# The triangular inverse of a gated DeltaNet head: four doubling levels moved from 96 by 96 products to 32 by 32 diagonal blocks

## What is computed

```python
    kk = jnp.einsum('bhncd,bhnsd->bhncs', k, k)
    A = jnp.where(strict, beta[..., :, None] * kk * decay_mat, 0.0)
    rhs = jnp.concatenate([v * beta[..., None], k * (beta * jnp.exp(gam))[..., None]], axis=-1)
    sol = lax.linalg.triangular_solve(A, rhs, left_side=True, lower=True, unit_diagonal=True)
```

```python
    for gi in range(N_EXPERT_GROUPS):
        hdn = (jax.nn.silu(jnp.einsum('nd,edf->nef', xt, w_gate[gi]))
               * jnp.einsum('nd,edf->nef', xt, w_up[gi]))
        hdn = hdn * comb[:, gi, :, None].astype(hdn.dtype)
        y = y + jnp.einsum('nef,efd->nd', hdn, w_down[gi])
```

## Time and profile before

| | us |
|---|---|
| median of 3 runs | 849.45 (849.22 to 850.07) |
| the profiled execution, its own time | 850.3 |
| its span, first to last instruction | 848.6 |
| PE busy in the span | 786.8 |
| DVE, ACT, POOL busy | 327.2, 309.3, 132.0 |

### The profile page before, as it was taken

One profiled execution on the slowest core, in us unless ns is written; L12 is line 12 of the kernel. 1 busy time (PEld: TensorE's weight loads), 2 busy tenths in 40 slices (PEclk: granted clock), 3 DMA queues, 4 the chain that ended last, 5 costly groups with the idle time before them and its releaser, 6 DMA issues.

```text
span 848.6 us, 14904 instructions
## 1 busy us (share of the span) xinstructions
PE 786.8 (93%) x5989; PEld 581.5 (69%) x5989; DVE 327.2 (39%) x735; ACT 309.3 (36%) x593; POOL 132.0 (16%) x148
## 2 busy tenths in 40 slices
PE   3889999999999999999999999999999888988885
PEld 2778999999999999746556565565655554554542
DVE  3462777768675775327111221112211121121112
ACT  4561755776665646313212212121221211112123
POOL 3172262243156234200000000000000000000000
PEclk9885999999999999999999999999999999999998
DMA  9413434233514432689999999999999999999992
GB/s 321 121 51 100 112 100 112 76 89 85 152 28 117 119 103 75 248 328 410 422 427 425 421 429 422 428 424 423 429 421 429 422 427 423 427 426 422 427 419 119
DMA packets 84091, 240.99 MB, mean 284 GB/s; under 512 B 7089, under 2 KB 65570, under 8 KB 67506
## 3 DMA queue, kind: packets, MB, share of 16 engines
q1 hardware_dynamic: 83554, 238.34, 71.9%
q10 hardware_dynamic: 464, 1.64, 0.5%
HBM read 238.92 MB, written 1.05 MB: 283 GB/s over the span
## 4 chain that ended last, share of the span: by engine, by line
PE 74%; DMA 15%; SPq 3%; ACT 2%; DVE 2%; issue 2%; POOL 0%; ACTq 0%; DVEq 0%; POOLq 0%
PE banks L1616 20%; PE banks L1911 18%; DMA ring<-in_expert_w_up_dram 14%; PE banks L1962 10%; PE banks L1792 3%; PE banks L1922 3%; PE banks L1853 3%; PE banks L1724 2%; PE banks L1726 2%; PE banks L1707 2%; SPq L635 2%; SPq L641 1%; ACT bench L972 1%; PE banks L1673 1%; PE banks L1779 1%
## 5 line engine op out<-in xcount | busy, mean ns | idle before, releaser
L1911 PE MATMUL banks<-ring,bench 128*64 128x256 f32 x2048 | 229.8, 380 | 16.6 <-DMA ring<-in_expert_w_up_dram 10.6
L1911 PEld LDWEIGHTS banks<-ring,bench 128*64 128x64 f32 x2048 | 150.5, 137 | 104.8 <-issue 26.0
L1616 PE MATMUL banks<-rounded 128*128 128x272 f32 (+2 forms) x1368 | 207.3, 302 | 2.9 <-DVE rounded L1190 2.8
L1616 PEld LDWEIGHTS banks<-rounded 128*128 128x128 f32 (+1 forms) x1368 | 181.7, 194 | 6.3 <-DVE rounded L1190 3.0
L1962 PE MATMUL banks<-ring,bench 128*64 128x512 f32 x512 | 116.9, 599 | 11.6 <-ACT bench L972 11.6
L1530 DVE TENSOR_TENSOR bench<-banks,bench 128x256 f32<-128x256 f32 x32 | 13.6, 425 | 244.5 <-PE banks L1911 181.5
L1962 PEld LDWEIGHTS banks<-ring,bench 128*64 128x64 f32 x512 | 34.0, 137 | 74.0 <-issue 54.5
L983 ACT ACTIVATE ysb<-banks 64x512 f32<-64x512 f32 x63 | 37.2, 591 | 119.4 <-PE banks L1962 118.6
L972 ACT ACTIVATE bench<-banks 128x256 f32<-128x256 f32 x32 | 12.3, 383 | 180.1 <-PE banks L1943 180.1
L773 ACT ACTIVATE rounded<-room 128x1024 fp32r<-128x1024 f32 x56 | 58.6, 1052 | 14.8 <-PE banks L1616 14.7
L1190 DVE TENSOR_TENSOR rounded<-room,rounded 128x1024 fp32r<-128x1024 f32 x42 | 55.4, 1321 | 17.4 <-ACT rounded L773 16.2
(11 more groups left out here) (270 smaller groups left out, 960.1 us busy)
## 6 DMA issues: line engine op xcount, KB each, us to landing
ring<-in_expert_w_gate_dram SPq DMA_DIRECT2D x32, 2048.0 KB, 30.9
ring<-in_expert_w_down_dram SPq DMA_DIRECT2D x64, 1024.0 KB, 29.4
ring<-in_expert_w_up_dram SPq DMA_DIRECT2D x31, 2048.0 KB, 32.1
room<-in_w_in_dram SPq DMA_DIRECT2D x56, 512.0 KB, 3.8
ring<-in_w_out_dram SPq DMA_DIRECT2D x8, 512.0 KB, 4.3
ring<-in_expert_w_up_dram SPq DMA_DIRECT2D x2, 1024.0 KB, 36.9
x<-in_x_dram ACTq DMA_DIRECT2D x2, 512.0 KB, 4.6
poolw<-in_pool_w_dram SPq DMA_DIRECT2D x4, 256.0 KB, 4.2
```

The costliest lines, as they stand in the source:

```text
L1616: ins = T.matmul(o, a, b[:, k, lo_at:L], start=(k == 0 and n == 0), stop=(k == KT - 1 and n == 2))
L1911: ins = T.matmul(pb[5 + c][half * 64:half * 64 + SLOTS, 0:256], xgT[:, q % ROOMS, kt, j * SLOTS:(j + 1) * SLOTS], w[:, kt, half * 256:(hal ...
```

## The change

The levels 2, 4, 8 and 16 only ever touch the three 32 by 32 blocks on the diagonal of each 96 by 96 matrix. The change keeps those blocks alone, stacked on the partitions: partitions 0 to 31, 32 to 63 and 64 to 95 hold the first, second and third diagonal block of a chunk, and a chunk takes 32 columns instead of 96.

- `AT`, `at`, `tb` and `ub` go. Instead ACT copies the diagonal blocks of A (step `ac`, three instructions of 32 by 96), and DVE makes the first T and, with a transpose of 32 by 32 blocks, its transpose U (step `base`, three instructions of 96 by 96).
- A level of the first four is now: POOL masks 96 by 96 elements instead of 96 by 288; PE forms `W` in nine 32 by 32 matmuls, three chunks times three blocks, each on its own diagonal quadrant of the array; ACT copies 96 by 96; PE forms the transpose of Y (`YT`) in nine such matmuls; DVE adds it to U (step `uc`) and transposes the sum to get T (step `tf`). Y itself is no longer formed.
- At level 16 `uc` writes the blocks into the full U, and levels 32 and 64 need one product `W`, one `YT`, one copy (`uc`) and, for level 32, one transpose (`tf`).
- The planner's costs are changed with the steps, and the orders come out anew.
- POOL makes more constants at the start, and clears two buffers.

No DMA is added or taken away, and SP's order is the same.

```diff
+LEVEL = 0.43
...
-            op(("X", h, lv), "pe", 0.51 if big else 0.2 if lv == 4 else 0.33,
-               when(("mask", h, lv) if big else None, ("tb", h) if lv == 0 else ("ty", h, lv - 1)), due(h, left - 1), gets=("X", h, lv))
+            op(("W", h, lv), "pe", LEVEL if inner else 0.2, when(("mask", h, lv) if inner else None, ("base", h) if lv == 0 else ("uc", h, min(lv - 1, 3))), due(h, left - 1), gets=("W", h, lv))
...
+                    for r in range(3):
+                        rows = slice(32 * r, 32 * r + 32)
+                        nc.scalar.activation(Ac[rows, h % 2], Ab[rows, h % 2, :, rows], ACT.Copy).then_inc(S("ac"), 1)
...
+            for r in range(3):
+                rows = slice(32 * r, 32 * r + 32)
+                chain(nc.gpsimd.tensor_copy(blows[rows, 0, :], mlow[rows, rows]))
+                chain(nc.gpsimd.tensor_copy(blows[rows, 1:1 + MASKED, :], lows[rows, :, rows]))
+                chain(nc.gpsimd.tensor_copy(unit[rows, :], ident[rows, rows]))
+            for t in (Uf, Th):
+                chain(nc.gpsimd.memset(t, 0.0))
...
-                nc.gpsimd.tensor_tensor(OTb[:, h % 2, lv % 2], ATb[:, h % 2], mup[:, 1 + lv:2 + lv, :].to_broadcast([CH, NC_, CH]), ALU.mult).then_inc(S("OT"), 1)
+                nc.gpsimd.tensor_tensor(Ob[:, h % 2, lv % 2], Ac[:, h % 2], blows[:, 1 + lv:2 + lv, :].to_broadcast([CH, NC_, 32]), ALU.mult).then_inc(S("OT"), 1)
...
-                    chain(V.tensor_tensor(tmpT[:, 0], Ab[:], spread(mlow), ALU.mult))
+                    chain(V.tensor_tensor(Tmp[:, 0], Ac[:, h % 2], blows[:, 0:1, :].to_broadcast([CH, NC_, 32]), ALU.mult))
...
+                    chain(V.tensor_tensor(Tc[:, h % 2], Tmp[:, 0], unit.rearrange("p (o t) -> p o t", o=1).to_broadcast([CH, NC_, 32]), ALU.add))
+                    V.transpose(out=Uc[:, h % 2], in_=Tc[:, h % 2]).then_inc(S("base"), 1)
...
+                    if lv < 3:
+                        takes(V.tensor_tensor(Uc[:, h % 2], c3(p[0:CH, 0:CH]), Uc[:, h % 2], ALU.add), ("YT", h, lv))
...
+                    if lv < 3:
+                        ins = V.transpose(out=Tc[:, h % 2], in_=Uc[:, h % 2])
...
+            def per_block(key, product):
+
+                p = bank(pe, key)
+                for c in range(NC_):
+                    for r in range(3):
+                        rows = slice(32 * r, 32 * r + 32)
+                        ins = product(p[rows, c * 32:(c + 1) * 32], c, rows)
+                fills(ins, key)
...
-                if kind == "AT":
-                    h = step[1]
-                    taken(pe, ("G", h))
-                    per_chunk(("AT", h), CH, CH, lambda o, c: T.transpose(o, Ab[:, c, :], ident[0:CH, 0:CH]))
...
-                        per_chunk(("X", h, lv), CH, CH, lambda o, c: T.matmul(o, OTb[:, h % 2, lv % 2, c, :], Tb[:, h % 2, c, :], start=True, stop=True))
+                        per_block(("W", h, lv), lambda o, c, rows: T.matmul(o, Ob[rows, h % 2, lv % 2, c, :], Uc[rows, h % 2, c, :], start=True, stop=True, skip_group_check=True))
...
-                    if lv < MASKED and kind == "Y":
-                        per_chunk(("Y", h, lv), CH, CH, lambda o, c: T.matmul(o, Ub[:, h % 2, c, :], Xb[:, h % 2, c, :], start=True, stop=True))
-                    elif lv < MASKED:
-                        per_chunk(("YT", h, lv), CH, CH, lambda o, c: T.matmul(o, Xb[:, h % 2, c, :], Ub[:, h % 2, c, :], start=True, stop=True))
+                    if lv < MASKED:
+                        per_block(("YT", h, lv), lambda o, c, rows: T.matmul(o, Tc[rows, h % 2, c, :], Wc[rows, h % 2, c, :], start=True, stop=True, skip_group_check=True))
```

More of the change, by code:

```diff
@@ L345 @@
 OT_AT = {step[1:]: n + 1 for n, step in enumerate(s for s in SEQ_OF["pool"] if s[0] == "mask")}
+TF_AT = {step[1:]: n + 1 for n, step in enumerate(s for s in SEQ_OF["dve"] if s[0] == "tf")}
 LO_AT = {}
@@ L1329, in _ @@
+                if kind == "tf":
                     h, lv = step[1:]
-                    b = LEVELS[lv]
-                    q = filled(dve, ("YT", h, lv))
-                    if lv < MASKED:
-                        takes(V.tensor_tensor(Ub[:, h % 2], c3(q[0:CH, 0:LP]), Ub[:, h % 2], ALU.add), ("YT", h, lv))
-                    else:
-                        takes(V.tensor_copy(Ub[0:b, h % 2, :, b:b + 32], c3(q[0:b, 0:LP])[:, :, b:b + 32]), ("YT", h, lv))
+                    taken(dve, ("YT", h, lv))
+                    if lv < 3:
+                        ins = V.transpose(out=Tc[:, h % 2], in_=Uc[:, h % 2])
+                    elif lv == 3:
+                        if h >= 2:
+                            filled(dve, ("YT", h - 2, 5))
+                        for r in range(2):
+                            rows = slice(32 * r, 32 * r + 32)
+                            ins = V.transpose(out=Th[rows, h % 2, :, rows], in_=Uf[rows, h % 2, :, rows])
+                    else:
+                        ins = V.transpose(out=Th[32:64, h % 2, :, 0:32], in_=Uf[0:32, h % 2, :, 32:64])
+                    ins.then_inc(S("tf"), 1)
@@ L1708, in _ @@
                     else:
-                        p = bank(pe, ("X", h, lv))
-                        for c in range(NC_):
-                            ins = T.matmul(p[b:b + 32, c * CH:c * CH + b], ATb[0:b, h % 2, c, b:b + 32], Tb[0:b, h % 2, c, 0:b],
-                                           start=True, stop=True, skip_group_check=True)
-                        fills(ins, ("X", h, lv))
-                if kind in ("Y", "YT"):
+                        b = LEVELS[lv]
+                        low, diag = slice(0, b), slice(b, b + 32)
```

161 lines of the change are left out of this document (73 added, 88 removed).

## The result

| | before | after |
|---|---|---|
| median of 4 runs, us | 849.34 (847.32 to 850.07) | 818.72 (816.84 to 821.12) |
| profiled execution: time, span, us | 850.3, 848.6 | 820.57, 818.8 |

The ratio is 0.9645 (interval 0.9607 to 0.9682): 30.6 us faster, where the sum of the forecast had 12.7. The sign came out as predicted and so did the mechanism of the middle stretch. The size did not, the reading of the first head did not either, and the time lies outside the range.

What follows compares the result with a forecast made beforehand. The prediction took PE to pace the mixers and the weight stream to keep the experts' stage's length. Its terms, 11.9 + 2.5 - 1.7 = 12.7 us, taken from 849.45, gave 837 us, with 828 to 851 for 8 in 10.

Steps and rivals of the forecast that it cites:

- PE bounds the middle: From 90 to 357 us PE is full, so a microsecond less PE work is close to a microsecond less time.
- The price of a small group: Eighteen records on three quadrants cost PE 0.60 us, between 0.50 and 0.68; a head saves 2.0 us.
- The share of 85%: Seven heads where PE is full: of 14.0 us saved, 11.9 get through, because smaller groups have waits with less filling.
- The first head: A chain through DVE, ACT and PE before the middle stretch; shorter copies and additions save 2.5 us, between 1 and 4.
- a risk of the other sign: Clock rival, 3%: thinner products could keep PE at the low clock into the second head, cost 10 us, leave 847 to 852.
- Minus 1.7 for the output step ahead of `m`: At the mixers' end, four more output projection records stand ahead of step `m`, so SP is let go 1.7 us later.
- SP's queue: SP's issues around step `m`: no new wait and no new DMA, counted at nothing.
- Thin overlap: Rival, 13%: records of different quadrants start no closer than about 0.023 us, a group is 0.78; 3.6 us saved, 846.
- No overlap for the shared PSUM bank: Rival, 12%: quadrants writing one bank take turns, a group is 0.86 us; about 1 us slower, 850.5.
- Drains at each quadrant: Rival, 5%: each change of quadrant drains the array, a group is 1.66 us, the kernel near 895.

Runs made afterwards that it cites:

- Doubled: Against the changed kernel, every small product of the first four levels is made twice into the same place; 833.1 us, ratio 0.9829.
- blockwise: Against the changed kernel, the two loops are turned, so all six records of a quadrant stand one behind the other; 828.74 us, ratio 0.9778.
- with a third product: Against the changed kernel, quadrants stay but Y is formed again at levels 2, 4 and 8 and added instead of transposing; 825.48 us, ratio 0.9721.

## Why the prediction was wrong in size

- **PE bounds the middle, and its saving arrives: right.** Doubled, blockwise and with a third product, the middle grew by 13.1, 9.0 and 5.2 us, as the groups' own prices say; 16 us on the chains beside it cost 1.6.
- **The price of a small group: at its bound.** I took 0.60 between 0.50 and 0.68, and it is 0.51, with 0.20 for going in and out as read in the earlier trace rows. The other prices held. A head then saves 2.7 us instead of 2.0, some 5 us more in seven heads.
- **The share of 85% was the step that I chose and did not read, and it failed.** Nothing was lost at the smaller groups: PE's waits at them are 2.3 us in the span. With the 1.7 us of the moved output step, which are inside the 19.3, the seven heads gave 21.0 us, 3.0 a head, against 2.7 by the prices. The 2.1 us between are less than what another order alone moves; their place stays open.
- **The first head, 2.5 between 1 and 4, measured 10.0: this is the term that failed most.** I read it as a chain and put PE's own part at nothing ("hardly changes"). But PE was busy 41.79 of 46.00 us there, and 2.3 us added to the chain did nothing visible. I had seen the clock of 0.74 and used it only as a risk of the other sign. Low clock is (1 - 0.74) times 60 us, 15.6 us of full-speed work lost before, 10.2 after: 5.4 us of the ten, as an estimate at its upper bound (the rate from run to run is 0.7 to 0.8 of that); PE's own work of one head is another 2.7, and 1.9 are left for the rest. In the kernel before, raising the clock with added products moved tile 8 by 8.4, of which up to some 3.6 may be the choice of the two profiles. So the clock has the largest part in this profile. In the medians it goes with 6 to 7 us, by the estimate above. How the rest of the first stretch divides stays open.
- **Minus 1.7 for the output step ahead of `m`: as computed, not measured apart. SP's queue:** after `m` it gave 1.1 us, where I had counted none.
- **The whole gap.** The profiles differ by 29.8 us and the sum had 12.7. Of the 17.1 between, the first head has 7.5, the price of a group 5.0, the share 2.1, the open place in the middle 2.1 and SP with the end 0.6; the rest is rounding.
- **The rivals.** Thin overlap needs starts 0.023 apart; they are 0.011. The Trainium skill (TensorE: Matmul & The Clock Gate, "Wait — 56ns, not 53.3ns?") has them never closer than about 25 ns; across quadrants this trace does not agree. No overlap for the shared PSUM bank does not show either: three quadrants write one bank and a group is 0.51, not 0.86. The Trainium skill (TensorEngine Tiling (Array Packing), "Gotcha 1: PSUM Pressure") has different row tiles unable to access one bank at one time; for these three, each writing its own partitions of the bank, this trace does not agree. Drains at each quadrant would have made a group 1.66 us; it is 0.51. The Trainium skill (TensorEngine Tiling (Array Packing), "Key Properties") has a change of tiling mode, not of tile, drain the engine; the 0.20 us of going in and out, with nothing visible between quadrants, agrees.

## What to carry to other kernels

Where a stretch has PE at 99% of its time, count PE's start-to-start distances with what they cost their neighbours, and pass the whole saving on; a discount needs a wait in the trace that would eat it. Where the granted clock of a stretch is under 1, ask first what the edit does to the clock, and count PE's own work too: here that was worth more than any step of the chain. Take the two halves of such a change apart by themselves before you say which one pays: here either alone brought more than half of the middle. Where small products stay, let the records of different quadrants take turns. Before comparing two stretches, count what work the order has put into each.

## What was not expected of the hardware

- Three diagonal quadrants of 32 by 32 writing one PSUM bank start 0.011 us apart, with no loss against one quadrant alone. At the low clock (from 55 to 64 us in the changed kernel) there are 0.30 us from first to last start, not twice the 0.19.
- The order of the same eighteen records alone moves their starts from 0.19 to 0.36 us.
- Products that compute nothing made the kernel before faster (845.3 against 847.84), with the clock from 30 to 90 us at 0.97 instead of 0.74.
- A lone small group costs 0.51 us for 18 records, and a lone wide one 0.55 for six, so at this size a smaller product alone gains little. A second small group beside the first costs 0.25, where a second wide one costs 0.5: going in and out is 0.20 us of a lone small group.
